# Block outputs finished by groups of tokens, the modulation on four column tiles, the decays' chain reordered, and the convolution's low parts on GpSimd

## The reference, cut to what matters

```
h = concat(meta, x)                                  # 272 x 1024
# layer 0
gate, xr = split(h @ rg_w_in)                        # 2 x 1344
xc = conv_b + sum_tap shift(xr, tap) * conv_w[tap]   # 4 taps
r, i = sigmoid(xc @ w_gates + b)                     # block diagonal
y = scan(a(r), u(r, i, xc)) * gelu(gate)
h = layer_norm(ALPHA * h + y @ rg_w_out)             # "first end"
h = layer_norm(ALPHA * h + swiglu(h))                # 3584 wide; "second end"
# layer 1, gated linear attention in chunks of 64 tokens
q, k, v, r, z = split(h @ gla_w_in)
log_g = log_sigmoid(z @ w_gate_up + b) / 16 ; b = cumsum over a chunk
E1..E4 = exp of differences of b ("decays"), multiplied onto q and k
o = norm(intra-chunk + state part) * silu(r)
h = layer_norm(ALPHA * h + o @ gla_w_out)            # "third end"
h = layer_norm(ALPHA * h + experts(h))               # top 2 of 8
# layer 2
mod = silu(c) @ w_ada + b_ada                        # 1 x 6144: sh1, sc1, g1, sh2, sc2, g2
```

## Time and profile before

| | us |
|---|---|
| median of 3 runs | 2119.68 (2116.54 to 2120.32) |
| profiled execution | 2118.84 |
| its span | 2117.1 |
| TensorE busy in the span | 1875.7 (89%) |
| VectorE, ScalarE, GpSimd busy | 614.2, 498.8, 351.5 |

### The profile page before, as it was taken

One profiled execution on the slowest core, in us unless ns is written; L12 is line 12 of the kernel. 1 busy time (PEld: TensorE's weight loads), 2 busy tenths in 40 slices (PEclk: granted clock), 3 DMA queues, 4 the chain that ended last, 5 costly groups with the idle time before them and its releaser, 6 DMA issues.

```text
span 2117.1 us, 29243 instructions
## 1 busy us (share of the span) xinstructions
PE 1875.7 (89%) x12245; PEld 1106.1 (52%) x12245; DVE 614.2 (29%) x1209; ACT 498.8 (24%) x892; POOL 351.5 (17%) x306
## 2 busy tenths in 40 slices
PE   8888999997698599999999999999994875689996
PEld 7876999665695333323332333233322865544442
DVE  6665655334444700100000000010005565421102
ACT  4833444314332201000100010000003543321220
POOL 3000000000000099999930000000001000000000
PEclk9997999996898699999999999999996877879998
DMA  5536555355534499999999999999994430459995
GB/s 175 146 105 217 182 177 180 128 170 187 164 100 139 153 408 411 408 418 410 411 406 418 411 411 401 419 410 410 403 389 137 131 112 1 161 232 419 419 419 217
DMA packets 203443, 583.09 MB, mean 275 GB/s; under 512 B 11161, under 2 KB 101930, under 8 KB 176672
## 3 DMA queue, kind: packets, MB, share of 16 engines
q1 hardware_dynamic: 200688, 575.09, 71.2%
q0 software_dynamic: 2608, 5.97, 1.0%
HBM read 579.96 MB, written 1.05 MB: 274 GB/s over the span
## 4 chain that ended last, share of the span: by engine, by line
PE 66%; DMA 13%; DVE 11%; ACT 6%; issue 2%; SPq 1%; POOL 0%; ACTq 0%; DVEq 0%; POOLq 0%
PE ps L1626 16%; PE ps L443 8%; PE ps L445 7%; PE ps L444 7%; DMA ring<-in_moe_w_out 7%; PE ps L2059 5%; PE ps L1631 4%; PE ps L1662 4%; DMA ring<-in_moe_w_in 3%; PE ps L2083 3%; DVE wlo L476 2%; ACT whi L468 2%; SPq L1474 1%; PE ps L1667 1%; PE ps L2044 1%
## 5 line engine op out<-in xcount | busy, mean ns | idle before, releaser
L1626 PE MATMUL ps<-ring,xg 128*64 128x512 f32 x1624 | 410.7, 600 | 13.1 <-ACT sgm L1736 5.8
L476 DVE TENSOR_TENSOR wlo<-raw,whi 128x2048 fp32r<-128x2048 f32 (+6 forms) x97 | 213.8, 2208 | 295.3 <-ACT whi L468 295.1
L443 PE MATMUL ps<-xh,whi 128*128 128x272 f32 (+1 forms) x712 | 215.1, 302 | 25.5 <-DVE E L1341 16.8
L1626 PEld LDWEIGHTS ps<-ring,xg 128*64 128x64 f32 x1624 | 121.5, 137 | 219.3 <-issue 207.8
L468 ACT ACTIVATE whi<-raw 128x2048 fp32r<-128x2048 f32 (+6 forms) x97 | 178.8, 1845 | 225.9 <-PE ps L445 114.9
L1662 PE MATMUL ps<-ring,ahm 128*64 128x512 f32 x824 | 204.5, 597 | 11.6 <-DMA ring<-in_moe_w_out 10.6
L445 PE MATMUL ps<-xh,wlo 128*128 128x272 f32 (+1 forms) x712 | 212.2, 298 | 0.0
L444 PE MATMUL ps<-xl,whi 128*128 128x272 f32 (+1 forms) x712 | 211.9, 298 | 0.0
L672 POOL DMA_DIRECT2D lnt<-in_ln_gain x4 | 2.2, 554 | 1184.3 <-issue 525.8
L1992 POOL TENSOR_SCALAR lnt<-lnt,h 128x384 f32<-128x384 f32 x120 | 188.6, 1572 | 12.2
L1800 DVE TENSOR_TENSOR sgm<-sgm,ps 128x512 f32<-128x512 f32 x28 | 18.2, 684 | 513.3 <-PE ps L1631 513.3
(11 more groups left out here) (555 smaller groups left out, 2531.9 us busy)
## 6 DMA issues: line engine op xcount, KB each, us to landing
ring<-in_moe_w_in SPq DMA_DIRECT2D x203, 1024.0 KB, 18.0
ring<-in_moe_w_out SPq DMA_DIRECT2D x103, 1024.0 KB, 19.9
ring<-in_w_gate SPq DMA_DIRECT2D x29, 1024.0 KB, 13.5
raw<-in_ffn_w_in SPq DMA_DIRECT2D x28, 1024.0 KB
ring<-in_w_down SPq DMA_DIRECT2D x26, 1024.0 KB, 12.7
raw<-in_w_ada SPq DMA_DIRECT2D x24, 1024.0 KB
more<-in_moe_w_in SPq DMA_DIRECT2D x21, 1024.0 KB, 18.1
ring<-in_w_up SPq DMA_DIRECT2D x20, 1024.0 KB, 11.3
```

The lines of the kernel that those rows point to most:

```text
L443: e.matmul(o, lh, rh, start=start, stop=False)
L476: e.tensor_tensor(wlo[0:rows, s % NSPL, 0:n], raw[0:rows, i % NRAW, 0:n], whi[0:rows, s % NSPL, 0:n].bitcast(F32), ALU.subtract).then_inc( ...
L1626: e.matmul(ps_[b][64 * v:64 * v + 64, :], a[:, kk_, 64 * v:64 * v + 64], both[v][:, k, 512 * b:512 * b + 512], start=kk_ == 0, stop=kk_ == 7)
```

## The change

- **Ends.** The last two chunks of each output product are taken together (`pe_last_two`): first the meta rows, then all four blocks of 128 rows for token tile 0, then for tile 1. `dve_ln_tiles` makes sums, statistics and inverse root for meta rows and tile 0 as one group, for tile 1 as another; ScalarE norms the first group, does one `split_hi` (at the third end the modulation row), and norms half of tile 1, VectorE the other half. `pe_turn_tiles` transposes the first group's parts of six steps ahead.
- **Modulation.** A chunk is now 256 rows by 1024 columns; four chunks form a group that sums in one held bank over four column tiles. One row copy, one pair of column matmuls and one VectorE addition for each group. The 24 chunks lie at other places: 0 and 1 ahead of the last two chunks of `ro`, 2 and 3 behind the first feed-forward pair, 4 to 7 behind pairs 4, 6, 8 and 10, 8 and 9 ahead of the last two chunks of the second product, 10 to 15 among k and q, 16 to 19 ahead of x3, 20 and 21 ahead of the last two chunks of `go`, 22 and 23 behind them.
- **Decays' chain.** ScalarE does the exps E1 to E3 ahead of q0's high half; VectorE does k's products for both chunks ahead of the next low half, and the first low half behind E1.
- **Small loads.** The gate bias and the norm's gain are issued at tile 1's last product, the gate weights at the last transpose, the router's weights in layer 0.
- **Convolution.** The 12 low parts move from VectorE to GpSimd, behind its memsets.
- **Splits.** At the first two ends one chunk fewer is split ahead when the next stage begins.

```diff
@@ plan
-            M.add(("ada", j), 128, CW, by_rows(w_ada, 256 * j, 8, 256), split=False)
+            part = w_ada[256 * (j % 4):256 * (j % 4) + 256, 1024 * (j // 4):1024 * (j // 4) + 1024]
+            M.add(("ada", j), 128, CW, by_rows(part, 0, 2, 1024), split=False)
...
-FFN_ADA = (3, 6, 9)
+FFN_ADA = (4, 6, 8, 10)
...
-    plan_ada(3)
     M.add(("gz", 0), 128, 128, by_rows(w_gl, 3072, 8, 16))
-    plan_ada(1)
-    M.add(("gk", 0), 128, CW, by_rows(w_gl, 512, 8, 256))
-    plan_ada(1)
-    M.add(("gk", 1), 128, CW, by_rows(w_gl, 768, 8, 256))
-    plan_ada(2)
+    for j in range(2):
+        M.add(("gk", j), 128, CW, by_rows(w_gl, 512 + 256 * j, 8, 256))
+        plan_ada(2)
     for j in range(2):
         M.add(("gq", j), 128, CW, by_rows(w_gl, 256 * j, 8, 256))
         plan_ada(2 - 2 * j)
-    plan_ada(1)
...
-    for j in range(4):
-        plan_ada((3, 1, 0, 0)[j])
+    for j, n in enumerate((0, 2, 2, 2)):
         M.add(("go", j), 128, CW, by_blocks(d["gla_w_out"][0], j, 128))
-    plan_ada(3)
+        plan_ada(n)
+    plan_ada(2)
@@ new functions
+    def pe_ada(e, j):
+        g, r = j // 4, j % 4
+        w = weights(e, M, ("ada", j)).rearrange("p (k n) -> p k n", k=2)
+        p = bank("ada", g) if r else bank.take(e, "ada", g)
...
+        for k in range(2):
+            for c in range(4):
+                ins = e.matmul(p[32 * c:32 * c + 32, 0:256], silp[:, 2 * r + k, :], w[:, k, 256 * c:256 * c + 256],
+                               start=r == 0 and k == 0, stop=r == 3 and k == 1)
...
+    def pe_last_two(e, key, acc, front, wkeys, x, meta):
+        w = [[a.rearrange("p (i n) -> p i n", i=2) for a in weights(e, M, k)] for k in wkeys]
+        for i, parts in enumerate(meta):
+            ins = pe_meta_rows(e, front, wkeys[i], parts)
...
+        for t, n, cc in XTILES:
+            for m in range(4):
+                wh, wl = w[m // 2]
+                for q in range(2):
+                    o = slice(512 * q, 512 * q + 512)
+                    ins = mm3(e, acc[t, q][:, :], *x(m, cc, n), wh[:, m % 2, o], wl[:, m % 2, o], False, m == 3)
+            ins.then_inc(pe.s, pe.up((key, "tile", t), *(used(M, k) for k in wkeys)))
...
+    def act_ln_tiles(e, key, first, between):
+        e.wait_ge(dve.s, dve.at(key, "stat", 0))
+        for t, n, _ in first:
+            c = place[t]
+            e.activation(h[0:n, t, :], h[0:n, t, :], ACT.Identity, bias=..., scale=...)
+        between()
+        e.wait_ge(dve.s, dve.at(key, "stat", 1))
+        e.activation(h[:, 1, 0:512], h[:, 1, 0:512], ACT.Identity, bias=..., scale=...)
...
+    def pe_turn_tiles(e, key, norm, tiles, nk, ahead):
...
+        e.wait_ge(act.s, act.at(norm, "norm", 0))
+        for k in range(ahead):
+            first(k)
+        e.wait_ge(act.s, act.at(norm, "norm", 1))
+        e.wait_ge(dve.s, dve.at(norm, "norm"))
+        for k in range(nk):
+            if k >= ahead:
+                first(k)
+            t, n, c = tiles[-1]
+            e.transpose(p[k][:, c:c + n], src_h(t, k), idn[0:n, 0:n]).then_inc(pe.s, pe.up((key, "T", k)))
@@ pool_setup, dve_rg
+        for m in range(12):
+            e.wait_ge(act.s, act.at("xc", m))
+            e.tensor_tensor(xcl[:, m, :], X2[:, m, :], xch[:, m, :].bitcast(F32), ALU.subtract)
...
-            if m:
-                behind(m - 1)
-        behind(11)
@@ pe_rg (the second and third product likewise)
-            if j == 3:
-                pe_modulation(e, 0, 2)
-        pe_modulation(e, 2, 2)
-        pe_turn(e, "x1", src_h, TILES, 8)
+        for j in range(2):
+            pe_ada(e, j)
+        pe_last_two(e, "ln0", acc, front, [("ro", 4), ("ro", 5)], ...)
+        pe_turn_tiles(e, "x1", "ln0", TILES, 8, 6)
@@ pe_gla
-        pe_modulation(e, 17, 4)
+        for j in range(16, 20):
+            pe_ada(e, j)
         e.wait_ge(dve.s, dve.at("og"))
         pe_turn(e, "x3", lambda t, k: on[:, t, 128 * k:128 * k + 128], XTILES, 8)
@@ act_gla
-        act_modulation(e, 12, 2)
-        split_hi(e, M, s)
-        s += 1
+        act_ada(e, 2)
         e.wait_ge(dve.s, dve.at("dec"))
...
         e.activation(fl(E3), fl(bb), ACT.Exp, scale=1.0 / 16).then_inc(act.s, act.up(("E3",)))
+        split_hi(e, M, s)
+        s += 1
@@ pool_gla
-        for s in (pe, act, dve):
-            e.wait_ge(s.s, s.at("end_ffn"))
-        pool_ln(e, 1)
+        e.wait_ge(pe.s, pe.at("ln1", "tile", 1))
         e.dma_start(bgr[:, :], ...)
         e.dma_start(ngb[:, :], ...)
+        e.wait_ge(pe.s, pe.at("end_ffn"))
+        e.dma_start(wgu, d["gla_w_gate_up"][0])
+        for s in (act, dve):
+            e.wait_ge(s.s, s.at("end_ffn"))
+        pool_ln(e, 1)
```

More of the change, by code:

```diff
@@ L643, in dve_ln @@
+    def dve_ln(e, key, tiles):
         e.wait_ge(dve.s, dve.n)
@@ L829, in pe_rg @@
         front = bank.take(e, "ln0", 2)
-        for j in range(6):
+        for j in range(4):
             wh, wl = (w.rearrange("p (i n) -> p i n", i=2) for w in weights(e, M, ("ro", j)))
@@ L1146, in pe_tokm, with pe_rows_out @@
             bank.give((key, j, t), (act, key, j, t))
-    def pe_rows_out(e, key, acc, tiles, tx, between=(None,) * 4):
-        for j in range(4):
-            if between[j] is not None:
-                between[j](e, 0)
+    def pe_rows_out(e, key, acc, tiles, tx, chunks):
+        for j in range(chunks):
             wh, wl = (w.rearrange("p (i n) -> p i n", i=2) for w in weights(e, M, (key, j)))
@@ L1160, in pe_rows_out @@
             ins.then_inc(pe.s, pe.up((key,), used(M, (key, j))))
-            if between[j] is not None:
-                between[j](e, 1)
     def pe_gla(e):
```

296 lines of the change are left out of this document (155 added, 141 removed).

## The result

The changed kernel took 2105.08 us (median of 4 runs, 2104.61 to 2106.16) against 2120.0 for the kernel before (2116.54 to 2121.43) in the same job. The ratio is 0.9933, with a 95% interval of 0.9916 to 0.995: faster by 14.9 us by the medians. I had said 2096. The profiled execution took 2106.16 with a span of 2104.3, where before had 2117.1: 12.8 us shorter, against 23.3 forecast.

What follows compares the result with a forecast made beforehand. Before a DMA-bound stretch from about 720 us, the chain of TensorE's work and waits was taken as the bound. Terms 1.8 + 0.4 + 1.4 - 4.5 - 6.4 - 19.7 + 0.5 + 3.2 = -23.3 gave 2096 us, range 2084 to 2108.

Steps and rivals of the forecast that it cites:

- the likeliest case: Whole kernel: the eight terms sum to -23.3 us, time 2096, own range 2091 to 2101; chance 0.49.
- Conv low parts: Convolution: subtractions on GpSimd slow VectorE by a third of their overlap, 2.7, less 0.9 gained: +1.8 us.
- First end: End of layer 0's output product: joint wait for the last two chunks, slow clock, shorter tail: +0.4 us.
- feed-forward: Feed-forward stretch: more modulation work on saturated TensorE, +2.3, less 0.9 from a shorter silu wait: +1.4 us.
- second end: End of the feed-forward's second product: same joint wait, but tail no longer behind five modulation chunks: -4.5 us.
- start of the attention layer: Before the gate matmuls: small loads issued earlier, so the 6.7 us wait ends: -6.4 us.
- q and k: Gate matmuls to first v product: both 8.4 us waits on the decays' products go: -19.7 us.
- Third end: End of layer 1's output product: transposes stand behind modulation 18's load, first product +5.5; whole end +3.2 us.
- the transposes aren't held by modulation: Third end: -5.5 us, part of a rival where the ends do better, 2085.5; chance 0.15.
- the port lock: Convolution: each GpSimd operation stops VectorE for its full length, costing 7.3 instead of 1.8: 2101.5; chance 0.17.
- the 2104 of a kept wait of 8.4 us in q and k: q, k stretch: q1 or q0 still waits behind its load, +8.4 us: 2104; chance 0.13.
- The loads of 11 us: Six places where TensorE waits behind a load: 11 instead of 5.3 us each, 34 us: 2130; chance 0.06.

Runs made afterwards that it cites:

- after: The changed kernel itself, with all parts of the change, against the kernel before: 2105.08 us, ratio 0.9933.
- The fill: Changed kernel plus extra matmuls while TensorE waits, 22 ahead of q0 and 18 ahead of the per-head output's state: 2102.93 us.
- the one version built on it: The kernel before with only the convolution's 12 low parts moved to GpSimd: 2123.35 us.
- The best version: Changed kernel with low parts on VectorE, modulation 18 to 21 moved later, only the last chunk by token tiles, extra matmuls at q0, per-head output and gates: 2074.28 us.
- the version with the modulation behind the turn: Changed kernel with modulation 18 and 19 behind the first chunk of layer 1's output product, 20 and 21 behind its products: 2092.93 us.
- the two versions above: Changed kernel with extra matmuls before q0 and the per-head output, 2102.93 us; the same plus three edits and extra matmuls at the gates, 2074.28 us.
- the last version: The 2074.28 us kernel with 52 and 42 more extra matmuls at the first and second end, ahead of the transposes: 2074.34 us.

## Why the forecast was right in direction and too large by eight to ten

Eight of the ten steps went the way that the prediction said, and the range of 2084 to 2108 held the time; the likeliest case's own range, 2091 to 2101, did not. Of the 23.3 us, 8.4 are missing by the medians and 10.5 by the spans, in four places.

**Conv low parts: +1.8 forecast, +5.5 in the profiled execution.** This is the term that was mis-sized most. I scaled from a row that lost a third, a form with one tensor input, and took the third for the likelier case. VectorE lost 4.9 us beside 11 subtractions, where the third gave 2.7 and "in full" 8.2, so the right price lay between the two. The last conv sum came 2.8 later (68.00), since VectorE's earlier pauses took up part. The rest came behind it: TensorE waits 2.05 us at 61.91 for a low half that VectorE now makes too late, which no step of mine had, the clock is slow until 76.5 instead of 71.2, and at 130.90 there is a wait of 1.88 with a slow first chunk (7.4 us instead of 5.8). How much of this comes with the move differs from one execution to the next. Counted from the first conv instruction, the fourth chunk ends after 123.0 us before and 122.8 with the low parts back on VectorE. In the seven kept traces with the subtraction on GpSimd it is 126.2 to 126.4 in three, 127.2 and 127.5 in two, and 128.8 in two (after is one of these, and both have the wait of 1.9 at 130). So the move costs 3.2 to 5.8 there, by the state of the clock around it; the 5.5 is of an execution at the dear end. By the times the move costs 5.3 one way and 2.9 the other.

**First end, feed-forward, second end, start of the attention layer: right within 0.5 each.** 8.38 and 7.87 us of idling before the last 80 matmuls, 8.0 from their end to the turn (185.57 to 193.59, 487.00 to 495.02), the wait of 1.96 at the second product and no small load. But the right sum hid a poor trade: I had priced the joint wait for two chunks and accepted it, and did not ask what one chunk would do. It is 3.4 and 5.3 us better by the same reckoning.

**q and k: -19.7 forecast, -16.7.** q0 started 25.5 us behind the gate matmuls (25.2 forecast), with the 3.13 us wait that the sum contains. What it left out is that the clock falls in such a wait: q0 took 9.0 instead of 6.1. I had charged a slow clock to the waits of 8 us and to the third end, and none to this one.

**State and output per head: 0 forecast, +2.4.** Missed. VectorE's chain of states sets the start there, and TensorE now comes to it with its clock up and idles 2.54 us. The fill shows it: with the clock kept up the stage is 2.7 shorter.

**Third end: +3.2 forecast, +1.9.** The mechanism held to 0.2 us (first output product +5.3, forecast +5.5); the slow clock that I added behind it was not there. The prediction named the cure, in a rival only as "the transposes aren't held by modulation (-5.5)"; it was worth 10.7 in the trace and 12.2 in the time, since in the changed kernel the first product follows the gated output by 15 us and could follow by 4.

**The rest: 0 forecast, +2.1.** From the third end to the last products nothing moves (-0.3), and behind VectorE's last step 0.7 are gained. Between them that step begins 3.1 us later than it did, with no wait named. The changed kernel and the eleven versions built on it show 4.0 to 4.6 there, the kernel before and the one version built on it 1.40. The difference lies behind a jump, beside packets of the instruction queues. Why it is there in one program and not in the other stays open.

Of the rivals, the port lock named the right kind of cost, since the engines exclude each other, but not its size. The rival whose time came nearest to 2105.1, the 2104 of a kept wait of 8.4 us in q and k, was wrong in its mechanism: no such wait was there. The loads of 11 us did not come.

## What to carry to other kernels

Before an elementwise instruction with two inputs moves to GpSimd, look at what VectorE does at that time. If that has two inputs in SBUF too, count a loss on both sides: here each subtraction of 0.76 us took 0.4 to 0.5 from VectorE. Price a wait of TensorE not by its length alone; one of 2.5 to 3 us cost about as much again in what followed, and matmuls with no purpose, into a bank that is about to be overwritten, took that back where TensorE was the bound behind it. Where two things are queued on one engine and only the second is ready, swap them first: moving four unrelated chunks behind the transposes and products gave 12 us, nearly as much as the whole change. The best version, 2074.28, is 45.7 us or 2.2% below the kernel before, and 30.8 below the changed kernel.

## What the runs showed of the hardware

- Conv instructions of VectorE with two SBUF inputs and GpSimd's subtractions alternated, a pair in 0.93 to 0.97 us, where they take 0.50 and 0.76 apart. A conv instruction took 0.90 to 1.02 in such a pair. A copy on GpSimd lengthened VectorE's group of three by 0.15 at most and was itself lengthened from 0.41 to 0.62 to 0.70 beside conv instructions and up to 2.43 beside a low half.
- TensorE's granted clock fell to 1.2 GHz in or behind waits of 1.85, 1.88, 2.54 and 3.13 us, and the work that followed was longer by 1.6, 1.6, 2.7 and 2.7; behind waits of 0.4, 1.14 and 1.33 nothing was. The length of the wait does not settle it. The same wait of 3.7 us in the gate branch was followed by 8 us at a granted clock of 1.00 in the changed kernel (122.76) and of 0.79 in the kernel before (118.82), and the wait of 1.96 at the feed-forward's second product by 1.00 there (381.27) and by 0.79 in the version with the modulation behind the turn.
- With filler matmuls in the wait it stayed at 2.4 GHz (1.00 over 8 and 10 us) in the two versions above. In the last version the same 22 before q0 left a wait of 1.74, and the clock fell (0.79 over 517 to 525 us). In the turn, with pauses between short bursts, it fell although the wait before it had been filled.
- Behind a jump over a skipped part of the program VectorE's next instruction came after 3.1 to 3.7 us in twelve traces, each with four or five packets of the instruction queues in that time, and after 0.49 in two, without such packets.
